# Nine slots instead of six for the experts' weights

## The reference, cut to what matters

```
xt = rmsnorm_2(x, norm2_g).reshape(512, 1024)
g_idx  = argmax(xt @ w_rg + b_rg)                       # 4 groups
e_in   = (xt @ w_re + b_re)[group g_idx]                # 8 experts of that group
top_v, top_i = top_k(e_in, 2)
top_w  = softmax(top_v) * p_group
def expert_block(xb, e):
    return (silu(xb @ w_gate[e]) * (xb @ w_up[e])) @ w_down[e]
y[token] = sum over its two experts of top_w * expert_block(...)
```

## Time and profile before

| What | Value |
|---|---|
| Median of three runs | 1991.0 us (1988.43 to 1992.31) |
| Profiled execution, its own time | 1988.91 us |
| Its span | 1987.1 us |
| Mean granted TensorE clock | 0.967 |
| TensorE busy | 1827.0 us, 92% of the span |
| VectorE, ScalarE, GpSimd busy | 589.3, 336.2, 18.6 us |
| Moved by DMA | 335.34 MB, 169 GB/s over the span |

### The profile page before, as it was taken

One profiled execution on the slowest core, in us unless ns is written; L12 is line 12 of the kernel. 1 busy time (PEld: TensorE's weight loads), 2 busy tenths in 40 slices (PEclk: granted clock), 3 DMA queues, 4 the chain that ended last, 5 costly groups with the idle time before them and its releaser, 6 DMA issues.

```text
span 1987.1 us, 17326 instructions
## 1 busy us (share of the span) xinstructions
PE 1827.0 (92%) x6710; PEld 880.0 (44%) x6710; DVE 589.3 (30%) x1357; ACT 336.2 (17%) x681; POOL 18.6 (1%) x38
## 2 busy tenths in 40 slices
PE   6999999989999999989899888999979999999992
PEld 2445544434444444435344444444454544545540
DVE  4322435432222210130876233312241111111102
ACT  2112223221111100011233313320110000000000
POOL 0001000000000000000000000000000000000001
PEclk9999979999999999999899899999989999999996
DMA  9665020011222111232111101033139999999994
GB/s 393 247 254 190 1 85 1 32 72 47 80 84 84 63 72 58 87 116 85 47 43 43 43 0 43 0 127 127 52 162 413 429 428 429 429 428 429 429 428 167
DMA packets 30979, 335.34 MB, mean 169 GB/s; under 512 B 3192, under 2 KB 5768, under 8 KB 11600
## 3 DMA queue, kind: packets, MB, share of 16 engines
q1 hardware_dynamic: 23216, 310.56, 38.6%
q10 hardware_dynamic: 5312, 15.43, 2.0%
q0 software_dynamic: 2400, 8.65, 1.3%
HBM read 319.66 MB, written 18.37 MB: 170 GB/s over the span
## 4 chain that ended last, share of the span: by engine, by line
PE 74%; DMA 16%; DVE 5%; ACT 3%; issue 1%; POOL 0%; SPq 0%; ACTq 0%; DVEq 0%; POOLq 0%
PE bank L898 15%; DMA upper<-in_w_expert_up 14%; PE bank L539 10%; PE bank L557 8%; PE bank L1225 8%; PE bank L1020 5%; PE bank L989 3%; PE bank L1028 3%; PE bank L718 2%; PE bank L615 2%; PE bank L638 2%; PE bank L860 2%; PE bank L1234 2%; PE bank L979 2%; PE bank L625 1%; PE bank L708 1%
## 5 line engine op out<-in xcount | busy, mean ns | idle before, releaser
L1225 PE MATMUL bank<-slot,arena 128*64 128x512 f32 x1024 | 337.7, 595 | 26.4 <-DMA upper<-in_w_expert_up 24.0
L898 PE MATMUL bank<-hT,slot 128*128 128x512 f32 x704 | 304.1, 595 | 6.9 <-ACT hT L1985 6.9
L1225 PE MATMUL bank<-upper,arena 128*64 128x512 f32 x512 | 228.1, 599 | 0.0
L898 PEld LDWEIGHTS bank<-hT,slot 128*128 128x128 f32 x704 | 134.3, 191 | 176.7 <-issue 175.4
L1225 PEld LDWEIGHTS bank<-slot,arena 128*64 128x64 f32 x1024 | 104.8, 137 | 242.6 <-issue 206.5
L539 PE MATMUL bank<-arena,slot 128*128 128x512 f32 x352 | 152.9, 597 | 3.3 <-DVE arena L1629 3.3
L1020 PE MATMUL bank<-hT,slot 128*128 128x512 f32 x256 | 120.8, 620 | 12.0 <-ACT arena L1985 10.4
L1234 PE MATMUL bank<-arena 128*128 128x128 f32 x1024 | 123.0, 279 | 8.5 <-DVE arena L1909 8.5
L557 PE MATMUL bank<-hT,slot 128*128 128x512 f32 x272 | 122.9, 609 | 7.6 <-DVE hT L1659 6.5
L1234 PEld LDWEIGHTS bank<-arena 128*128 128x128 f32 x1024 | 118.7, 195 | 20.8 <-issue 20.8
L539 PEld LDWEIGHTS bank<-arena,slot 128*128 128x128 f32 x352 | 67.4, 192 | 88.8 <-issue 84.7
(11 more groups left out here) (354 smaller groups left out, 1745.9 us busy)
## 6 DMA issues: line engine op xcount, KB each, us to landing
slot<-in_w_expert_gate SPq DMA_DIRECT2D x32, 2048.0 KB, 16.8
upper<-in_w_expert_down SPq DMA_DIRECT2D x16, 2048.0 KB, 18.4
slot<-in_w_expert_down SPq DMA_DIRECT2D x16, 2048.0 KB, 13.9
slot<-in_w_expert_up SPq DMA_DIRECT2D x16, 2048.0 KB, 17.7
upper<-in_w_expert_up SPq DMA_DIRECT2D x16, 2048.0 KB, 23.0
slot<-in_w_in SPq DMA_DIRECT2D x15, 2048.0 KB, 7.8
slot<-in_w_ada SPq DMA_DIRECT2D x12, 2048.0 KB, 14.7
slot<-in_w_up SPq DMA_DIRECT2D x11, 2048.0 KB, 7.6
```

Of the source, the lines that this page charges most:

```text
L898: ins = pe.matmul(bank[4 * j + c][:, :], w[:, k, half:half + P], hT[:, k, :], start=(k == 0), stop=(k == KD - 1))
L1225: ins = pe.matmul(dst[b * CAP:(b + 1) * CAP, :], lhs(b, k), rhs(b, k), start=(k == 0), stop=(k == n_k - 1))
```

## The change

The ring grows to nine slots: the six of before and, as numbers 6, 7 and 8, `arena[4096:8192]` (where the squares were), `hT` and `xT`. The 96 slabs are numbered in the order of use (gate, gate, up, up, down, down for each pair); slab c goes into slot `turn9[c % 9]`, so a slot holds gates, ups and downs in turn. Slabs 6, 7 and 8 (the gates of experts 2 and 3, the up of expert 2) are issued once the route stage's last reader of each place is done. From then on slab c + 9 is issued when the products that read slab c are done.

Since 9 slots and 6 slabs a pair repeat after three pairs, the loops of SyncE and TensorE take three pairs a turn; TensorE's pairs 13, 14 and 15 are written out. Three more semaphores are needed, and some others are merged to make room (`ld_rel` into `ld_tab`, `ext1_w` and `ld_T1` into `bias1`, `ext2_w` and `ld_T2` into `bias2`, `ld_gm` into `ld_small`).

```diff
         ws = [ring[0], ring[1], ring[2], ring[3], upper[:, 0:SLOT], upper[:, SLOT:2 * SLOT]]
+        ws += [arena[:, SLOT:2 * SLOT], hT.rearrange("p k t -> p (k t)"), xT.rearrange("p k t -> p (k t)")]
...
+        turn9 = (0, 3, 1, 4, 2, 5, 6, 7, 8)
...
                 load(("eu", 0), 1, up_of(0), dense(G_WO2 + 8))
                 load(("eu", 1), 4, up_of(1))
-                with sp.Fori(1, E // 2) as p:
-                    for b in range(2):
-                        sp.wait_ge(S["g_full"], p)
-                        sp.dma_start(ws[3 * b][:, :], gate_of(p * 2 + b)).then_inc(landed[3 * b], 16)
...
+                load("ring6", 6, gate_of(2), (S["ss_full"], 1))
+                load("ring7", 7, gate_of(3), (S["lg_full"], 4))
+                load("ring8", 8, up_of(2), (S["xk_full"], 2 * NT))
+                def next_slab(i, r):
+                    used, of = ("g_full", "uu_full", "yy_full")[r % 6 // 2], (gate_of, up_of, down_of)[(r + 9) % 6 // 2]
+                    at = turn9[r % 9]
+                    sp.wait_ge(S[used], i * 3 + (r // 6 + 1))
+                    sp.dma_start(ws[at][:, :], of(i * 6 + (2 * ((r + 9) // 6) + (r + 9) % 2)))\
+                      .then_inc(landed[at], 16)
+                with sp.Fori(0, 4) as i:
+                    for r in range(18):
+                        next_slab(i, r)
+                for r in range(15):
+                    next_slab(4, r)
...
-                pair(0, True, False)
-                with pe.Fori(1, E // 2 - 1) as p:
-                    pair(p, False, False)
-                pair(E // 2 - 1, False, True)
+                pair(0, [placed(0, c) for c in range(6)], first=True)
+                with pe.Fori(0, 4) as i:
+                    for q in range(1, 4):
+                        pair(i * 3 + q, [placed(i, 6 * q + c) for c in range(6)])
+                for p in range(13, E // 2):
+                    pair(p, [placed(0, 6 * p + c) for c in range(6)], last=(p == E // 2 - 1))
...
-            ve.wait_ge(S["ld_tab"], 16)
+            ve.wait_ge(S["ld_tab"], 32)
...
-                pe.wait_ge(S["ld_gm"], 16)
+                pe.wait_ge(S["ld_small"], 48)
...
-                ve.wait_ge(S["ld_T2"], 16)
+                ve.wait_ge(S["bias2"], 48)
```

More of the change, by code:

```diff
@@ L280, in two_blocks @@
         S = {n: sem(n) for n in names}
-        landed = [sem(f"landed{i}") for i in range(6)]
+        landed = [sem(f"landed{i}") for i in range(9)]
         gath = [sem(f"gathered{t}") for t in range(NT)]
@@ L322, in emptied @@
             return (S["act_free"] if who == "A" else S["dve_free"]), owners[:g + 1].count(who)
-        loads = [0] * 6
+        loads = [0] * 9
         ATT1 = [(h, q, 0, q + 1) for h in range(HEADS) for q in range(NT)]
@@ L1219, in _, with placed @@
                 base = [arrived[(n, b)][1] for b in range(2) for n in ("eg", "eu", "ed")]
+                base += [16] * 3
+                def placed(i, c):
+                    at = turn9[c % 9]
+                    return at, i * 32 + (base[at] + 16 * (c // 9))
                 def both_k(n_k, lhs, rhs, dst):
@@ L1242, in turn_inner, with pair @@
                     ins.then_inc(S["ht_full"], 1)
-                def pair(p, first, last):
+                def pair(p, at, first=False, last=False):
                     pe.wait_ge(S["xt_ev"], p * 2 + 2)
@@ L1247, in pair @@
                         for b in range(2):
-                            pe.wait_ge(landed[3 * b + half], p * 16 + base[3 * b + half])
+                            pe.wait_ge(landed[at[2 * half + b][0]], at[2 * half + b][1])
                         both_k(KD, lambda b, k: xsT[:, k, b * CAP:(b + 1) * CAP],
-                               lambda b, k: slot(3 * b + half, KD, EF)[:, k, :], bank[2 + half]).then_inc(S[full], 1)
+                               lambda b, k: slot(at[2 * half + b][0], KD, EF)[:, k, :], bank[2 + half]).then_inc(S[full], 1)
                     if not last:
@@ L1258, in pair @@
                     for b in range(2):
-                        pe.wait_ge(landed[3 * b + 2], p * 16 + base[3 * b + 2])
+                        pe.wait_ge(landed[at[4 + b][0]], at[4 + b][1])
                     pe.wait_ge(S["ht_ev"], p + 1)
@@ L1506, in _ @@
                 ve.wait_ge(S["a_exp"], 1)
-                ve.wait_ge(S["ext2_w"], 16)
+                ve.wait_ge(S["bias2"], 16)
                 ve.wait_ge(*emptied(G_Z + 3))
@@ L2033, in _ @@
             rr = a["rel_rev"]
-            ac.dma_start(e1[:, 127:383], rr[:, 0:256]).then_inc(S["ld_rel"], 16)
+            ac.dma_start(e1[:, 127:383], rr[:, 0:256]).then_inc(S["ld_tab"], 16)
             ac.wait_ge(S["ld_cols"], 16)
@@ L2042, in _ @@
                 ac.dma_start(dst.rearrange("p k n -> p (k n)"), a[name]).then_inc(S["ld_small"], 16)
-            ac.wait_ge(S["ld_rel"], 16)
+            ac.wait_ge(S["ld_tab"], 32)
             act(e1[:, 0:127], e1[:, 127:128].to_broadcast([HEADS, 127]), ACT.Copy, "e1_rdy")
             own("e1_rdy")
-            ac.dma_start(ext1, e1).then_inc(S["ext1_w"], 16)
-            ac.wait_ge(S["ext1_w"], 16)
-            ac.dma_start(skew1, ext1.unsqueeze(0).to_broadcast([P, HEADS, 383])).then_inc(S["ext1_w"], 16)
+            ac.dma_start(ext1, e1).then_inc(S["bias1"], 16)
+            ac.wait_ge(S["bias1"], 16)
+            ac.dma_start(skew1, ext1.unsqueeze(0).to_broadcast([P, HEADS, 383])).then_inc(S["bias1"], 16)
             ac.wait_ge(S["ld_rows"], 16)
@@ L2051, in _ @@
             ac.wait_ge(S["e2_rdy"], 1)
-            ac.dma_start(ext2[:, :], e2[0:8, :]).then_inc(S["ext2_w"], 16)
+            ac.dma_start(ext2[:, :], e2[0:8, :]).then_inc(S["bias2"], 16)
             if on("proj"):
@@ L2080, in _ @@
                 silu(7)
-                ac.wait_ge(S["ext2_w"], 16)
-                ac.dma_start(skew2, ext2.unsqueeze(0).to_broadcast([P, HEADS, 512])).then_inc(S["ext2_w"], 16)
+                ac.wait_ge(S["bias2"], 16)
+                ac.dma_start(skew2, ext2.unsqueeze(0).to_broadcast([P, HEADS, 512])).then_inc(S["bias2"], 16)
             if on("ssd"):
@@ L2111, in _ @@
                 rows_in(3)
-                ac.wait_ge(S["ext1_w"], 32)
+                ac.wait_ge(S["bias1"], 32)
                 ac.dma_start(T1, bass.AP(tensor=skew1.tensor, offset=127, ap=[[HEADS * 383 - 1, P], [383, HEADS], [1, 256]]))\
-                  .then_inc(S["ld_T1"], 16)
+                  .then_inc(S["bias1"], 16)
                 ac.wait_ge(S["a_rdy"], 1)
@@ L2141, in _ @@
                 ac.wait_ge(*emptied(G_WA))
-                ac.dma_start(w_gm.rearrange("p k n -> p (k n)"), a["w_gm_2"]).then_inc(S["ld_gm"], 16)
+                ac.dma_start(w_gm.rearrange("p k n -> p (k n)"), a["w_gm_2"]).then_inc(S["ld_small"], 16)
                 for m in range(KD):
@@ L2182, in _ @@
             if on("proj2"):
-                ac.wait_ge(S["ext2_w"], 32)
+                ac.wait_ge(S["bias2"], 32)
                 ac.wait_ge(S["dn_full"], 8)
-                ac.dma_start(T2, bass.AP(tensor=skew2.tensor, offset=127, ap=[[HEADS * 512 - 1, P], [512, HEADS], [1, 384]])).then_inc(S["ld_T2"], 16)
+                ac.dma_start(T2, bass.AP(tensor=skew2.tensor, offset=127, ap=[[HEADS * 512 - 1, P], [512, HEADS], [1, 384]])).then_inc(S["bias2"], 16)
                 empties(G_QA, G_QM - G_QA)
@@ L2374, in _ @@
             ins.then_inc(S["consts"], 1)
-            po.wait_ge(S["ld_T1"], 16)
+            po.wait_ge(S["bias1"], 48)
             po.memset(T1[0:HD, :, 3 * HD:4 * HD], NEG).then_inc(S["t1_masked"], 1)
```

6 lines of the change are left out of this document (3 added, 3 removed).

## The result

| | Before | After |
|---|---|---|
| Median | 1990.42 us (1988.43 to 1992.31, 4 runs) | 1975.74 us (1974.15 to 1977.51, 4 runs) |
| Profiled execution, span | 1987.1 us | 1973.1 us |

The ratio is 0.9927 with a 95% interval of 0.9909 to 0.9944: 14.7 us faster by the medians, 14.0 us by the two spans. Forecast were 1976.3 us and 14.7 us.

What follows compares the result with a forecast made beforehand. The experts' weight stream was taken as the bound, idle in the stage ahead. Three slabs moved off it gave -14.7 us, all else 0: 1991.0 - 14.7 = 1976.3 us, own range 1973 to 1980, eight times in ten 1971 to 1984.

Steps and rivals of the forecast that it cites:

- Three slabs off the stream: Experts' weight stream: 87 slabs instead of 90 to move from 1478.7 us, so its end comes 14.7 us earlier.
- the small holes of 1478.7 to 1508 us stay: Weight stream after the first release: slots come free as before, so its small holes remain.
- The three fit in the idle stretch: Stream ahead of 1478.7 us: three early slabs end by about 1454, 1459 and 1464 us, 14 us to spare.
- TensorE's pace and its reserve: Expert pairs: TensorE paces 0 to 9, the stream 10 to 15; 11.6 us spare at pair 15, waits 10.9 us.
- the prediction's own sum: Pair n's up landing trails TensorE's pace by 1.85 + 2.04 (n - 3) us, less 14.7; positive from pair 10.
- Behind the last landing: Last down products after the final slab lands: left at 8.80 us, bounds 0 or 1.7 us less.
- the held clock: Rival at the kernel's end: shorter waits let the last down products take 7.1 us, giving 1974.6 us; 10%.
- The route stage and the merged semaphores: Ahead of the experts: loads beside VectorE's chain and raised semaphore counts were each to cost 0.
- The longer loop: TensorE's loop body grows from 84 to 252 matmuls (62 KB); taken as kept, cost 0, 38 instruction packets.
- The rival: TensorE's long loop is not kept and stops at three jumps; 1995.6 us at 10.3 us each; 4% for slower.
- the two-page window: Skill's rule on instruction fetch: a taken branch outside the current two-page window forces a fetch; would favour the long-loop rival.
- the store of 2048 instructions: Skill's figure for the PE's instruction store; the new body of about 1000 would fit, favouring the forecast.

Runs made afterwards that it cites:

- the extra work: The changed kernel with one extra matmul per expert ahead of every pair's gate and up products; 1991.03 us against 1975.53 for the change.
- six slots with more work: The kernel before with extra matmuls ahead of every pair's gate and up products; 1990.46 us, ratio 1.0.
- the longer loop: The changed kernel with TensorE's loop of six pairs run twice instead of three pairs run four times; 1976.93 us in one run.

## Why the prediction was right

**Three slabs off the stream, 14.7 us: right in the sum, not in its parts.** From before to the change the stream is shorter by 13.7 to 14.7 us, and the last landing moved from 1943.12 to 1929.06. With none early and three early, in the same ring, it takes 469.53 and 457.05 to 458.07 us: 11.5 to 12.5 us for the head start, which I had at 14.7. The ring's depth adds 2.2 us that I had put at 0 ("the small holes of 1478.7 to 1508 us stay"). The two errors nearly cancel, because they are one: a third slab that is not early fills the hole. The sum of three whole slabs holds against the kernel before, whose six slots leave the hole open; it is not what the head start is worth in the deeper ring. That the median came within 0.6 us is partly luck too, with runs that spread over 3 us. The holes do stay in the changed kernel, at 390 and 333 GB/s. The holes are also larger than their busy shares say: at 390 and 339 against 429 GB/s, 2.0 + 1.6 = 3.6 us of bytes are missing, against 1.8 us by the DMA share of 0.95 and 0.91. Some 1.4 us of it is the start of the stream, 131 GB/s in its first 2 us, which is there with seven slabs issued too (139 GB/s).

**The three fit in the idle stretch: right.** Issues at 1443.32, 1445.08 and 1450.09 us, forecast 1443.8, 1445.5 and 1450.5 (this execution was 0.4 us earlier as a whole); full until 1464.

**TensorE's pace and its reserve: right in kind, a little large.** The first wait for an up slab comes in pair 9 (0.46 us) and not in pair 10, and there are seven for ups instead of six. With the 13.7 us by which this trace's stream is shorter in place of 14.7 the prediction's own sum gives it: 1.85 + 2.04 x 6 - 13.7 = 0.4 us at pair 9. The waits for ups come to 11.6 us, with the last down to 13.3 and not 10.9. The reserve that I put at 11.6 us at pair 15 is confirmed by the extra work: 27.5 us of it cost 15.5, so 12.0 us were absorbed.

**Behind the last landing: the value was that of this one profile, not of the kernel.** 8.80 us came out in this execution, and with the semaphores alone and with more work on nine slots too. But the change once more, nine slots with none or two early, six slots with more work, and the longer loop all show 7.10 us after waits of 1.0 to 1.9 us. I gave the held clock 10%; it is closer to an even chance, and worth 1.7 us.

**The route stage and the merged semaphores: 0, as taken; SyncE: 0.35 us, taken as 0.** The route stage takes 29.57 us against 29.56, the semaphores alone give 0.9998. The first refill comes 7.67 us behind the first gate product instead of 7.32, at a time when the stream stands idle for it. Why is not shown.

**The longer loop: right, and nearer to the edge than it looked.** 38 instruction packets were forecast for a kept body, and 38 were measured. The rival needed two things: a body too long to keep, and 8.8 us a jump. The first is true at 123 KB and not at 62 KB; the second is not, the jump measured cost 2.01 us. Three such jumps, 6 us, would have been hidden by TensorE's reserve; with the lower clock behind each, 15.65 - 13.91 = 1.74 us more, they would have come to 11.3 us, just under it. So this rival deserved less than the 4% for slower. As for the Trainium skill, "Runtime: NRT & Kernel Launch", "Instruction fetch mechanics": of its two statements, the two-page window would have had the loop of three pairs (four packets) fetched again, and the trace shows none between 1620 and 1860 us; the store of 2048 instructions agrees with the kept body of an estimated 1000, and the body of an estimated 2000 was not kept although it is just under it.

## What to carry to other kernels

Where a stage is bound by its stream of weights, a slab fetched in an idle stretch ahead of it is worth up to its whole transfer time (here 4.8 us of 4.89 for the first two), less what it would have filled of a hole if held back (the third: 1.8 to 2.8 us), and a deeper ring without that head start only what its holes hold (2.2 us). Read two numbers first: how much stream time stands idle ahead of the first release, and how far the engine that consumes the slabs is ahead at the last one; the gain ends where either is used up. A wait that is the last on the path is worth only the time by which its partner, here the other operand, is ready before it (0.8 us), which is less than the wait that a profile puts down to it (1.68 us).

## What the runs showed of the hardware

A loop of TensorE whose instructions take an estimated 62 KB is kept between rounds, one of 123 KB is fetched again (52 packets instead of the 42 that its length alone explains), and its one jump back cost 2.01 us under a full stream. After a wait for a slab of 1.5 to 2.3 us TensorE's granted clock falls to its lower level of 1.2 GHz on some occasions and not on others: in the change's trace 32 products took 8.80 us instead of 7.10 behind the last wait of 1.7 us, while those behind the wait of 2.1 us that ended at 1766.15 us took 7.09. The window of 2 us in which the clock was down (its columns: length, TensorE busy and count, granted clock, DMA share, GB/s):

```profile
1930.00:1932.00 2.00, 2.00 (x8) 0.50 0.00 0
```

Eight products in 2 us, where the windows at the upper level hold twelve.
